# Order of work in a first layer: small loads, token transposes, two native fp32 quarters, gate sums, decay rows

## What is computed

```python
sh1_l, sc1_l, ... = jnp.split(jax.nn.silu(c) @ ada_w[i] + ada_b[i], 6, axis=-1)   # modulation, the same with c_ctx
hl = modulate(rms_norm(xl, norm_mix[i]), sh1_l, sc1_l)       # 256 tokens
hc = modulate(rms_norm(xc, norm_mix[i]), sh1_c, sc1_c)       # 256 context tokens
proj = h @ w_in                                              # q, k, v, z, gates, pool
qkv = silu(dw_conv(qkv, conv_w)); q, k = l2norm(q), l2norm(k)
beta = sigmoid(gates[:2]); log_decay = -exp(a_log) * softplus(gates[2:] + dt_bias)
o_f, o_b = gated_delta_chunked(...)                          # both directions, context state first
groups = [centred_mean(pg, ..., w) - pg for w in (2, 4, 8, 16)]
y = concat([rms_norm(o) * silu(z), groups @ pool_w * pool_scale]) @ w_out
x = x + g1 * y;  x = x + g2 * expert_choice_ffn(...)         # 16 experts
```

## Time and profile before

| What | before |
|---|---|
| median of three runs | 1434.03 us |
| the profiled execution, whole | 1432.99 us |
| its span, first to last instruction | 1431.2 us |
| TensorE busy (matmul) | 1194.1 us, 83% |
| VectorE, ScalarE, GpSimd busy | 624.0, 432.4, 78.2 us |
| DMA moved | 338.65 MB, mean 237 GB/s |
| granted clock of TensorE, mean | 0.935 |

### The profile page before, as it was taken

One profiled execution on the slowest core, in us unless ns is written; L12 is line 12 of the kernel. 1 busy time (PEld: TensorE's weight loads), 2 busy tenths in 40 slices (PEclk: granted clock), 3 DMA queues, 4 the chain that ended last, 5 costly groups with the idle time before them and its releaser, 6 DMA issues.

```text
span 1431.2 us, 19546 instructions
## 1 busy us (share of the span) xinstructions
PE 1194.1 (83%) x8265; PEld 887.2 (62%) x8265; DVE 624.0 (44%) x1136; ACT 432.4 (30%) x777; POOL 78.2 (5%) x118
## 2 busy tenths in 40 slices
PE   5899898998986556669999655666999999999887
PEld 3677567785852113139986211313899878899756
DVE  3645775646430001136653000112995456545574
ACT  2436333322310000034331000002554554443562
POOL 3000123540000000000000000000000000000000
PEclk9999899999989889889999988988999979999898
DMA  9845844426589999994549999999245303444000
GB/s 327 293 154 176 295 166 164 141 68 239 208 341 409 409 409 409 409 341 152 194 181 364 410 409 409 409 409 354 68 170 176 118 1 130 165 177 174 5 1 30
DMA packets 125099, 338.65 MB, mean 237 GB/s; under 512 B 8657, under 2 KB 11590, under 8 KB 125014
## 3 DMA queue, kind: packets, MB, share of 16 engines
q1 hardware_dynamic: 117536, 334.51, 61.6%
q10 hardware_dynamic: 7478, 2.91, 0.8%
HBM read 336.35 MB, written 1.05 MB: 236 GB/s over the span
## 4 chain that ended last, share of the span: by engine, by line
PE 59%; DMA 25%; DVE 10%; ACT 3%; issue 1%; ACTq 1%; SPq 1%; DVEq 0%
PE bank L685 9%; PE bank L687 9%; PE bank L686 9%; DMA expert_slots<-in_w_up_dram 7%; DMA weight_ring<-in_w_down_dram 6%; DMA arena<-in_w_gate_dram 4%; DMA arena<-in_w_up_dram 3%; DVE arena L1879 3%; PE bank L974 3%; DMA weight_ring<-in_w_gate_dram 3%; PE bank L592 2%; PE bank L1140 2%; PE bank L550 2%; PE bank L812 2%; PE bank L664 1%
## 5 line engine op out<-in xcount | busy, mean ns | idle before, releaser
L685 PE MATMUL bank<-input_high,weights_high 128*128 128x256 f32 (+1 forms) x992 | 290.8, 293 | 7.5 <-DVE input_low L1879 7.5
L686 PE MATMUL bank<-input_low,weights_high 128*128 128x256 f32 (+1 forms) x992 | 284.0, 286 | 0.0
L687 PE MATMUL bank<-input_high,weights_low 128*128 128x256 f32 (+1 forms) x992 | 283.9, 286 | 0.0
L1879 DVE TENSOR_TENSOR weights_low<-weight_ring,weights_high 128x1024 fp32r<-128x1024 f32 x144 | 176.1, 1224 | 182.4 <-ACT weights_high L1435 182.0
L685 PEld LDWEIGHTS bank<-input_high,weights_high 128*128 128x128 f32 x992 | 188.6, 190 | 12.8 <-issue 9.9
L1435 ACT ACTIVATE weights_high<-weight_ring 128x1024 fp32r<-128x1024 f32 x144 | 151.7, 1055 | 143.4 <-PE bank L687 143.1
L686 PEld LDWEIGHTS bank<-input_low,weights_high 128*128 128x128 f32 x992 | 188.2, 190 | 0.8
L687 PEld LDWEIGHTS bank<-input_high,weights_low 128*128 128x128 f32 x992 | 188.7, 190 | 0.0
L1879 DVE TENSOR_TENSOR arena<-arena,bank 128x512 f32<-128x512 f32 (+1 forms) x38 | 24.8, 652 | 275.8 <-PE bank L974 245.8
L974 PE MATMUL bank<-weight_ring,arena 128*32 128x512 f32 x480 | 68.5, 705 | 48.0 <-DMA weight_ring<-in_w_up_dram 25.9
L974 PEld LDWEIGHTS bank<-weight_ring,arena 128*32 128x32 f32 x480 | 15.9, 120 | 96.3 <-issue 39.9
(11 more groups left out here) (410 smaller groups left out, 1722.4 us busy)
## 6 DMA issues: line engine op xcount, KB each, us to landing
weight_ring<-in_ada_w_dram SPq DMA_DIRECT2D x24, 2048.0 KB, 8.9
weight_ring<-in_w_gate_dram SPq DMA_DIRECT2D x20, 2048.0 KB, 21.2
weight_ring<-in_w_down_dram SPq DMA_DIRECT2D x16, 2048.0 KB, 23.7
arena<-in_w_up_dram SPq DMA_DIRECT2D x12, 2048.0 KB, 24.2
arena<-in_w_down_dram SPq DMA_DIRECT2D x12, 2048.0 KB, 23.8
expert_slots<-in_w_up_dram SPq DMA_DIRECT2D x10, 2048.0 KB, 24.7
weight_ring<-in_w_up_dram SPq DMA_DIRECT2D x10, 2048.0 KB, 23.8
weight_ring<-in_even_w_in_dram SPq DMA_DIRECT2D x9, 2048.0 KB, 8.2
```

What stands on the lines that cost most here:

```text
L685: pe.matmul(b[:, 0:width], hi[:, k, :], XHI[:, k, t0:t0 + width], start=k == 0, stop=False)
L686: pe.matmul(b[:, 0:width], hi[:, k, :], XLO[:, k, t0:t0 + width], start=False, stop=False)
L687: mm = pe.matmul(b[:, 0:width], lo[:, k, :], XHI[:, k, t0:t0 + width], start=False, stop=k == KD - 1)
L1879: return dve.tensor_tensor(out_, a, b, op)
```

## The change

- **Small loads.** Six vector loads are issued after the first exponent, four after the first two squares, seven after the root; three small loads follow the meta tokens. The last four small loads are issued in `experts(0)`, after the softmax exponent, and `salog`'s exponent moves to `experts(1)`.
- **Tokens and modulation.** Tokens are turned after the first modulation product, then three more follow. The meta tokens and the later vectors are turned after the q product.
- **q product.** Its first two quarters are native fp32 matmuls of the unrounded weights with `hT`, paced by VectorE's scaling. ScalarE, not VectorE, scales the context half, and rounds it from the unscaled values. In `stream` the k chunk moves ahead of modulation chunk 4, the v chunk ahead of 5 and 6. Warm-up 4 in place of 10.
- **Gate sums** after the second pool quarter, with VectorE's part in group 1; **decay rows** turned right after the pool product, low part ahead of the token copies; pool sums of group 3 after the first "rows"; GpSimd's `ROW_OF` waits for `l2_done` 8 and no longer for `gam_args`.

The core of the diff:

```diff
-    steps = ada + [("turnrows", 0, 0, 0), ("rows", 0, 0, 0)]
+    steps = ada + [("rows", 0, 0, 0), ("poolsum", 0, 3, 0)]
...
-        n_small = len(small_src)
+        n_small = 3
...
-        for src, adas in (((ev, 0), 1), ((ev, 512), 1), ((ev, 1024), 1), ((ev, QKV), 0), ((ev, QKV + 512 + 16), 3)):
-            W_EV.append(len(stream))
-            stream += [cols(*src)]
-            for _ in range(adas):
-                ada_at.append(len(stream))
-                stream += [ada_src[len(ada_at) - 1]]
+        for src in ((ev, 0), (ev, 512), None, (ev, 1024), None, None, (ev, QKV), (ev, QKV + 512 + 16), None, None, None):
+            (ada_at if src is None else W_EV).append(len(stream))
+            stream += [ada_src[len(ada_at) - 1] if src is None else cols(*src)]
...
             ada_mm()
-            ada_mm()
-            pe.wait_ge(scalar_drained, ada["copied"] - 1)
-            ada_turn()
...
-            for i in range(2):
+            for i in range(3):
                 ada_mm()
                 pe.wait_ge(scalar_drained, ada["copied"] - 1)
                 ada_turn()
...
+            def late_vectors():
+
...
-                for m in range(4):
+                if i == 0:
+                    arrive(cn)
+                    for m in range(2):
+                        b = opener()
+                        for k in range(KD):
+                            if m == 0:
+                                pe.wait_ge(h_scaled, k + 1)
+                            mm = pe.matmul(b[:, 0:T], chunk(cn)[:, k, m * P:m * P + P], hT[:, k, 0:T], start=k == 0, stop=k == KD - 1)
+                        closer(mm, (names, mt + m))
+                for m in range(0 if i else 2, 4):
...
-                        if j in (0, 4):
-                            pe.wait_ge(first_split, KD * (j // 4) + k + 1)
+                        if (i, m) in ((0, 2), (1, 0)):
+                            pe.wait_ge(first_split, KD * i + k + 1)
...
+                        between(m)
+                released[cn] = (weights_split, len(quarters)) if i else (scalar_filled, done)
...
-            warm(10)
+            warm(4)
             first_product(0, 0, T, s_open, s_close, "qkv")
+            late_vectors()
             ada_step()
             first_product(1, 4, 2 * T, s_open, s_close, "qkv")
             ada_step()
...
-            first_product(4, 0, T, v_open, v_close, "pool", between=ada_step)
+            def after_pool(m):
+
+                if m == 1:
+                    pe.wait_ge(decay_ready, 1)
+                    b = v_open()
+                    for d in range(2):
+                        pe.matmul(b[:, 16 * d:16 * d + 16], (LE, GE)[d][:, :], G[:, :, 4 * d:4 * d + 4], start=True, stop=True)
+                    v_close(pe.matmul(b[:, 32:64], ONES, G, start=True, stop=True), "gc")
+                ada_step()
+
+            first_product(4, 0, T, v_open, v_close, "pool", between=after_pool)
...
+            pe.wait_ge(masks_ready, 4)
+            pe.wait_ge(gam_rows, 1)
             b = v_open()
-            for d in range(2):
-                pe.matmul(b[:, 16 * d:16 * d + 16], (LE, GE)[d][:, :], G[:, :, 4 * d:4 * d + 4], start=True, stop=True)
-            v_close(pe.matmul(b[:, 32:64], ONES, G, start=True, stop=True), "gc")
+            for u in range(UNITS):
+                mm = pe.transpose(b[0:SELROWS, u * P:u * P + P], GC2[:, u, :], ident[:, :])
+            v_close(mm, "gamma_rows")
...
-            pool.wait_ge(gam_args, 1)
+            pool.wait_ge(l2_done, 8)
...
+            load_vecs(later_vecs[:6])
...
                 if t == TT:
+                    load_vecs(later_vecs[6:10])
                     act.wait_ge(ctx_in, 16)
...
+            load_vecs(later_vecs[10:])
             act.dma_start(MIN[0:META, :], meta_2).then_inc(meta_in, 16)
-            load_vecs([name for name in vec_src if name not in first_vecs], vec_in)
-            for dst, src in small_src:
+            for dst, src in small_src[:n_small]:
...
             for tt in (1, 3):
...
+            for _ in range(3):
+                ada_copy()
+
+            for k in range(KD):
+                scaled_tiles[0] += 1
+                act.wait_ge(h_scaled, scaled_tiles[0])
+                act.activation(XHI1[:, k, 0:T], hT[:, k, 0:T], ACT.Copy).then_inc(h_ready, 1)
             high()
             high()
-            first_high(T, context_high)
-            act.wait_ge(small_in, 16 * n_small)
-            act.activation(alog, alog, ACT.Exp)
-            act.activation(salog, salog, ACT.Exp)
-            b = take()
-            drained(act.activation(XH[:, :, 0:META], bank(b, KD, META), ACT.Copy))
-
+            for half in range(2):
+                ks = range(4 * half, 4 * half + 4)
+                for k in ks:
+                    act.activation(XHI1[:, k, T:2 * T], hT[:, k, T:2 * T], ACT.Identity, scale=gain[:, k, 1:2],
+                                   bias=MOD[:, 0, k, 1:2]).then_inc(context_high, 1)
+                act.wait_ge(context_high, 4 * half + 4)
+                for k in ks:
+                    h = hT[:, k, T:2 * T]
+                    act.activation(h, h, ACT.Identity, scale=gain[:, k, 1:2], bias=MOD[:, 0, k, 1:2]).then_inc(context_scaled, 1)
+            high()
...
-                high()
+                if t >= 3:
+                    high()
+                if t == 3:
+                    b = take()
+                    drained(act.activation(XH[:, :, 0:META], bank(b, KD, META), ACT.Copy))
+                    act.wait_ge(small_in, 16 * n_small)
+                    act.activation(alog, alog, ACT.Exp)
...
+                if i == 2:
+                    high()
                 if i == 4:
-                    high()
                     ada_copy()
                     high()
+                    n["segment"] += 1
                     ada_copy()
-                    ada_copy()
-                    n["segment"] += 1
                     act.wait_ge(gam_args, 1)
                     for v in (EGC, KS, CDK):
                         ins = act.activation(v, GC if v is EGC else v, ACT.Exp)
                     ins.then_inc(gam_exps, 1)
+                    ada_copy()
+                    act.wait_ge(vector_filled, mark["gamma_rows"])
+                    act.wait_ge(l2_done, 4)
+                    b = VB[(mark["gamma_rows"] - 1) % 4]
+                    act.activation(ROWS[0:SELROWS, :], b[0:SELROWS, :], ACT.Copy).then_inc(rows_high, 1)
...
                 act.wait_ge(sm_args, ly + 1)
                 act.activation(AFFT, AFFT, ACT.Exp).then_inc(sm_exps, 1)
+                if ly == 1:
+                    act.wait_ge(ssd_small_in, 16 * (len(small_src) - n_small))
+                    act.activation(salog, salog, ACT.Exp)
+                else:
+                    for dst, src in small_src[n_small:]:
+                        act.dma_start(dst, src, allow_slow_non_contiguous=True).then_inc(ssd_small_in, 16)
...
+            for i in range(4):
...
+            for k in range(KD):
+                h = hT[:, k, 0:T]
+                dve.tensor_scalar(h, h, gain[:, k, 0:1], MOD[:, 0, k, 0:1], MUL, ADD).then_inc(h_scaled, 1)
             dve.memset(CB[:, :, :, 0:1], 0.0)
             dve.memset(CB[:, :, :, T + 1:T + 2], 0.0).then_inc(edges_ready, 1)
-            first_parts(1, context_high, (KD,))
+
+            def first_low(k, t0, signal):
+
+                dve.wait_ge(signal, k + 1)
+                tt(XLO1[:, k, t0:t0 + T], hT[:, k, t0:t0 + T], XHI1[:, k, t0:t0 + T].bitcast(F32), SUB).then_inc(first_split, 1)
+
+            for k in range(KD):
+                first_low(k, 0, h_ready)
+            split()
+            split()
+            for k in range(KD):
+                first_low(k, T, context_scaled)
             split()
...
+                if t >= 3:
+                    split()
+                if t == 6:
+                    dve.memset(PADP, 0.0)
...
-            for g in range(4):
...
-                drained(dve.tensor_copy(group[:, :, 8:72], bank(b, 4, 64)), True)
...
+            for g in range(4):
+                if g:
+                    ada_bias()
+                b = take()
+                drained(dve.tensor_copy(PADP[:, 4 * g:4 * g + 4, 8:72], bank(b, 4, 64)), g < 3)
+                if g < 2:
+                    split()
+                if g == 1:
...
+                    tt(GLB, GC, g_m[:, :, 8:16], SUB).then_inc(gam_args, 1)
                 l2_scale(g)
+                if g < 3:
+                    pool_sums(g)
+            n["segment"] += 1
...
             b = take()
...
+            dve.wait_ge(rows_high, 1)
+            low = ROWS[32:SELROWS, :]
+            drained(tt(low, b[32:SELROWS, :], low.bitcast(F32), SUB))
...
+                elif kind == "poolsum":
+                    dve.wait_ge(vector_drained, n["v"])
+                    pool_sums(h)
...
+                    if i == 0:
+                        dve.wait_ge(pooled_ready, 4)
```

112 lines of the change are left out of this document (32 added, 80 removed).

## The result

Over four runs the changed kernel took 1417.03 us (median; 1412.14 to 1422.48), before 1433.53 over four: a ratio of 0.9884, with a 95% interval of 0.9856 to 0.9912. The forecast was 1415.9 us in a range of 1412 to 1423. Five further rounds in another session gave 1418.29 against 1432.11, a ratio of 0.9904 (0.9879 to 0.993).

The account below looks back on a forecast made before the run. TensorE bounds 62 to 120 us; loads and ScalarE's issues hold the head, VectorE and GpSimd's select the tail. 1433.0 - 9.8 head - 8.8 tail + 0.5 experts = 1414.9, plus 1.0 for the median: 1415.9 us, range 1412 to 1423.

Parts of the forecast that it names:

- Tokens and product 3: Head: tokens start at 19.4 us, not 29.34; modulation product 3 at 34.3, not 37.77, taking the slow 3.64.
- q weights at 40.4 for lack of small packets: Head: without ScalarE's element loads the q weights land at 40.4 us, not 44.5.
- Native quarters: Head: two native quarters, 1.3 us costlier than split ones, end at 48.7; weight splits just make it, near 48.6.
- Second product at 57.7: Head: the second product starts at 57.7 us, not 67.5, a gain of 9.8 us.
- Tail -8.8: Tail, 155 to 184 us: earlier rows and a faster TensorE gain 9.2 us, less 0.4 charged for delayed pool sums.
- My end of -5.5: Tail: gain only 5.5 us if TensorE stays slow or VectorE's delay is passed on whole; 1419.2 us, chance 0.11.
- Pool sums under the select, .4: Tail: GpSimd's select delays the pool sums by 2.6 us on VectorE; 0.4 us charged.
- Experts +.5: Expert stage: packets of the four moved small loads meet a full DMA; 0.5 us charged, ends 0 and 4.2.
- its end of 4.2: Expert stage: the small loads cost their whole 4.2 us of bandwidth; 1419.6 us, chance 0.06.
- Rival (e): Experts: a full DMA holds up ScalarE's four issues; at 30 us of delay the kernel takes 1438; chance 0.04.
- Rival (d): Experts: their loads, not the layer before, set the end, so the gain doesn't arrive; about 1434 us, chance 0.04.
- The forecast of 18.1: Whole kernel: 18.1 us gained, from head -9.8, tail -8.8 and experts +0.5.

Follow-up runs that it names:

- e4: Kernel after with six warm-up matmuls on TensorE ahead of modulation product 3; the single run took 1407.06 us.
- e7: Kernel after with modulation product 1 and the turn of product 0 ahead of the tokens again; modulation product before the second product at 56.90 us against 56.79.
- e1: Kernel after with the four state-space loads issued at the head again, not at the experts; 1413.54 us against 1416.88 for the profiled kernel after.
- e2: Kernel after with the four state-space loads issued between ScalarE's copies of modulation products 2 and 3; modulation product before the second product at 58.11 us against 56.79.
- e11: Kernel after with state-space loads at the head, all q quarters split and modulation product 1 ahead of the tokens; the single run took 1428.92 us.
- e10: Kernel after with six warm-up matmuls, earlier GpSimd select, state-space loads on SyncE and third rounding behind the first quarter's copy; 1411.39 us, ratio 0.9878 to before.
- e5: Kernel after with gate sums, row turns and pool sum 3 at the tail put back; third decay rows at 162.74 us against 156.31.
- e6: Kernel after with GpSimd's fill and select started at the end of the pool product; fifth decay rows at 164.05 us against 163.09.
- e8: Kernel after with loads in ScalarE's gap, six warm-up matmuls, later third high part and earlier select; modulation product before the second product at 56.34 us against 56.79.

## Why the forecast came out, step by step

- **Tokens and product 3.** Right. Forecast 19.4 and 34.3, slow; measured 19.79 and 34.92, slow after a stand of 3.76 us, and fast where the stand was filled (e4). The order of tokens, which I told as a step of its own, is worth .1 (e7).
- **q weights at 40.4 for lack of small packets.** Right: they landed at 40.3, and e1 and e2 each make the slump again with the loads alone, e11 with the whole head undone. The Trainium skill (DMA: Bandwidth & Descriptors, Queues, rings and completion order) says that a DMA engine takes turns between the queues it has work for. From this I had concluded that no engine stands while weights wait; the share of .63 in e1 and e2 with weight loads outstanding disagrees with that conclusion. What in the four loads holds the engines stays open.
- **Native quarters.** Right in kind: split weights were done at 48.96 (46.61 + 2.35), just ahead of the end of the native quarters at 49.2 (42.17 + 7.07); forecast were 48.6 and 48.7.
- **Second product at 57.7.** Measured 58.7. Mis-sized was what I said of the context: ScalarE's sixteen operations took .52 each and not VectorE's .35, ended at 54.5 and not 53 (my own terms, 46 and 5.5, give 51.5), and TensorE stood .87 us for a bank copied behind them. e10 moved that copy: the stand is gone (.17 left elsewhere). A sum was wrong too: 34.3 + 3.64 + 2.8 + 0.3 is 41.0 for the first scaling and not 40.6. It came at 41.31, so the native quarters started .7 later than I said (42.17, not 41.5); with .87 for the stand that is 1.5 us. The native quarters gave .5 back (the next quarter began 6.7 us behind their start, not 7.2) and the late vectors .3; the two split quarters took .2 more.
- **Tail -8.8.** Measured -11.2 between M1 and R3 (176.34 - 156.31 less 8.8). The mechanisms were those named: the order (5.8, e5), q scalings without the select, and the clock. Too small were two terms. The stretch from the first to the third rows took 4.56 and not 5.1, and TensorE reached the first rows 7.8 us earlier in place of 6.3. Of the last 1.5 us, .5 had been gained ahead of the tail: the modulation product within the pool product, at 149.93 in before, came at 140.63, 9.3 us earlier and not 8.8. My end of -5.5 follows from no terms that I gave: a slow TensorE alone makes -6.3, VectorE's 2.6 passed on whole -6.6.
- **Pool sums under the select, .4.** Right (2.94 for one sum, .38 of standing, .5 back in e6). The Trainium skill (SBUF — State Buffer, SBUF: two separate sides) and the rows agree: two operands from SBUF are held, fill and bank copies are not.
- **Experts +.5.** Measured .3 to .4: E 30.36 against 30.06. But the term hides two of opposite sign. Small loads there cost some 1.6 us when TensorE has its full clock (E is 28.7 to 28.8 without them, in four runs; 30.1 to 31.1 with them, in five), and next to nothing when the gather runs slow (30.1 to 30.7 without, in three; 30.4 with, in two). Before ran slow and after did not. The forecast did not see that; its end of 4.2 was far.
- **Rival (e), ScalarE blocked.** Out: the issues took 2.2 us at the experts and 2.3 in the gap of e2, against 5.3 to 5.6 behind the queue of loads at the head.
- **The total.** Rival (d) is out: the gain reaches the experts, whose issue at 411.45 stood at 431.17 in before. At the issue of 580.40 the kernel is 19.6 us ahead of before (600.03), and 16.3 us at the end of the span. Of the 3.3 us lost behind 580, 2.7 fall in one stretch of unchanged code (940.57 to 1056.43, 115.9 us at a mean granted clock of .93; 113.1 at .95 in before). The forecast of 18.1 lies between. That the sum met within 1.1 us is partly luck: the head gained 1.0 less than I said, the tail 2.4 more, and 3.3 went behind 580.

How the clock moves the end needs a row. Windows of the kernel after and of e1, over the same code, which is 3.2 us later in e1:

```profile
308.00:312.00 4.00, 4.00 (x21) 0.94 (x20) 1.03 (x3) 0.06 (x1) 0.00 (x0) 0.57 0.03 10
```

```profile
308.00:312.00 4.00, 2.05 (x20) 1.61 (x24) 2.70 (x6) 0.00 (x0) 0.00 (x0) 1.00 0.87 331
```

The last columns are again granted clock, DMA share and GB/s. From the issue at 300.96 to that at 317.67 after takes 16.7 us and e1 15.1 (304.11 to 319.18): in one a stretch at a granted clock of .57 falls there, in the other none (mean .90 against 1.00). So e1, which is 3.9 us late at the head, ended 3.3 us ahead of after (1413.54 against 1416.88). A time of one run can't judge an edit of 2 us here; a marker near it can.

## What to carry to other kernels

Before moving small loads, look at what their packets do to the large transfers 6 to 12 us behind their issue, and at who would use the weights earlier: the 3.9 us appeared only since unsplit quarters could use them. A slot that costs nothing costs something once the work in front of it has become shorter. Judge each edit at a marker close behind it, not by the end of the run.

## What the runs showed of the hardware

- Four small loads, two of them of 4-byte elements, leave the 16 DMA engines at a share of .58 to .64 and 162 to 185 GB/s for some 8 us, 6 to 12 us behind the issue of the two D loads, while 2 MB loads wait (before, e1, e2, e8, e11; e8: .59 from 40 to 48). The three small loads that stayed at the head do not (1.05 throughout). Which of the four does it wasn't tried.
- ScalarE's Identity with a scale and a bias per partition took 0.52 us for 128x256, its plain copy 0.33.
- The issue of the pair of D loads took 1.4 us on an idle queue (after, e2, e8) and 3.7 to 4.1 behind a dozen others (before, e1, e11).
- The same later code (between SyncE's issues at 940.57 and 1056.43) took 115.9 us in after and 113.1 in before, e1 and e2.
- Six warm-up matmuls in the stand before modulation product 3 made it take 1.92 us (e4, e8, e10) in place of the 3.59 of after.
